# Two instruction streams in a two-layer decoder kernel: one for first halves of a sequence, one for second halves, with the boundary moved by 34 tokens

## The reference

```python
z = x @ w_in                       # q 1024, k 256, v 256, B 512, C 512, h 512, pool 512
a = sliding_window_attention(q, k, v)      # window 128, 16 heads, 4 kv heads, bias and sinks
c = B * causal_conv3(C * h)                # 512 channels
pm = (trailing_mean_2_4_8_16(p) - p) @ pool_w * pool_scale   # reaches 15 rows back
x = LN(alpha * x + concat(a, c, pm) @ w_o)
up = causal_conv3(x @ w_up)                # 2 x 5632 channels
x = LN(alpha * x + (silu(up[:, :5632]) * up[:, 5632:]) @ w_down)
```

## Time and profile before

| | us |
|---|---|
| Three runs | 3389.34, 2963.9, 3504.76 (median 3389.34) |
| The profiled execution, slowest core | 2965.69 |
| Its span, first to last instruction (core 6) | 2963.8 |
| PE busy in it | 2848.2 |
| DVE busy | 1536.0 |
| ACT busy | 962.4 |
| POOL busy | 533.3 |

### The profile page before, as it was taken

The page is one execution under the profiler, slowest core; times in us unless marked ns, Lnnn a source line. Parts: engine busy times, 40 slices in busy tenths (PEclk is TensorE's granted clock), DMA queues, the critical chain, the costliest instruction groups (busy, mean ns, idle before and its releaser), DMA issues.

```text
span 2963.8 us, 53483 instructions; the slowest of 8 cores (2954.7 to 2963.8 us)
## 1 busy us (share of the span) xinstructions
PE 2848.2 (96%) x18644; PEld 1767.7 (60%) x18644; DVE 1536.0 (52%) x3497; ACT 962.4 (32%) x2030; POOL 533.3 (18%) x764
## 2 busy tenths in 40 slices
PE   6999999999999999999999998989999999999995
PEld 3655555555555555555556555756666666666663
DVE  0366447655355435544562564476644563564456
ACT  1466126332033103301363663164311330331136
POOL 2131036100000000000072311261001001000026
PEclk9999999999999999999999999999999999999998
DMA  9522723534433343334448225534444434443434
GB/s 155 100 37 51 193 44 58 84 61 81 79 61 65 66 77 63 66 65 72 72 75 197 43 44 134 103 58 80 75 82 83 81 63 86 74 79 65 86 58 115
DMA packets 86887, 239.30 MB, mean 81 GB/s; under 512 B 11568, under 2 KB 32576, under 8 KB 86080
## 3 DMA queue, kind: packets, MB, share of 16 engines
q0 software_dynamic: 63488, 191.42, 38.7%
q1 hardware_dynamic: 23136, 44.46, 5.0%
HBM read 408.93 MB, written 20.75 MB: 145 GB/s over the span
## 4 chain that ended last, share of the span: by engine, by line
PE 92%; DVE 3%; ACT 2%; issue 1%; DMA 1%; POOL 1%; DVEq 0%; ACTq 0%; POOLq 0%
PE ps L194 92%; DVE xT L194 1%; DMA X<-xg 1%; DVE scr L194 1%; ACT xT L194 1%; ACT scr L194 1%; DMA slab<-w_in 0%; DVE H L194 0%; ACT rstd L194 0%; POOL H L194 0%; POOL xT L194 0%; DVEq L189 0%; DVE rstd L194 0%; ACT L194 0%; DVE small L194 0%
## 5 line engine op out<-in xcount | busy, mean ns | idle before, releaser
L194 PE MATMUL ps<-X,slab 128*128 128x386 bf16 (+6 forms) x10944 | 1747.8, 322 | 33.4 <-DMA slab<-w_in 13.7
L194 PEld LDWEIGHTS ps<-X,slab 128*128 128x128 bf16 x10944 | 1069.4, 98 | 694.7 <-issue 74.4
L194 PE MATMUL ps<-H,slab 128*128 128x384 bf16 (+2 forms) x5760 | 921.3, 319 | 0.0
L194 DVE SCALAR_TENSOR_TENSOR scr<-ps,fcw_s,scr 128x384 f32<-128x384 f32 (+2 forms) x1056 | 628.4, 596 | 406.3 <-ACT scr L194 349.2
L194 PEld LDWEIGHTS ps<-H,slab 128*128 128x128 bf16 x5760 | 564.6, 98 | 329.8 <-issue 2.9
L194 ACT ACTIVATE scr<-ps,fcw_s 128x384 f32<-128x384 f32 (+2 forms) x528 | 296.4, 563 | 1067.9 <-DVE ps L194 737.3
L194 DVE TENSOR_TENSOR xT<-xT,ps 128x384 f32<-128x384 f32 (+3 forms) x549 | 272.2, 531 | 216.1 <-PE ps L194 198.5
L194 POOL DMA_DIRECT2D slab<-w_up x176 | 94.1, 535 | 962.2 <-PE ps L194 960.4
L194 DVE TENSOR_TENSOR H<-scr 128x384 bf16<-128x384 f32 (+4 forms) x278 | 149.2, 539 | 105.7 <-ACT scr L194 76.8
L194 ACT ACTIVATE scr<-xT 128x384 bf16<-128x384 f32 (+2 forms) x192 | 96.8, 506 | 233.7 <-DVE xT L194 196.9
L194 POOL TENSOR_TENSOR H<-H,xT 128x384 f32<-128x384 f32 (+2 forms) x168 | 161.7, 962 | 35.4 <-DVE xT L194 23.8
(11 more groups left out here) (111 smaller groups left out, 938.6 us busy)
## 6 DMA issues: line engine op xcount, KB each, us to landing
slab<-w_up POOLq DMA_DIRECT2D x176, 512.0 KB, 7.7
slab<-w_dn POOLq DMA_DIRECT2D x96, 384.0 KB, 5.5
slab<-w_in POOLq DMA_DIRECT2D x56, 512.0 KB, 11.5
slab<-w_o POOLq DMA_DIRECT2D x32, 512.0 KB, 8.3
xT<-xr SPq DMA_DIRECT2D x16, 580.0 KB, 11.1
xT<-spill SPq DMA_DIRECT2D x16, 516.0 KB, 11.9
slab<-w_dl POOLq DMA_DIRECT2D x16, 512.0 KB, 7.6
xT<-gtab SPq DMA_DIRECT2D x4, 1024.0 KB, 14.0
```

The costliest lines, as they stand in the source:

```text
L194: bi = getattr(engobj, name)(*a_, **k_)
```

## The change

The program is built twice, as `program(0)` for first halves and `program(1)` for second halves, each with its own geometry (a tuple `Geo`, from `geometry(half)`). Each engine loads the word `flag` (0 or 1) from memory at the start and runs one of its two streams. Both streams use the same semaphores and the same tiles.

- **First halves** (even cores): 1058 own tokens instead of 1024. No history is computed: columns start at 256 (`BASE`), groups are 256-640, 640-1024 and 1024-1318 (384, 384, 294 columns) in both layers, also for K. V blocks are 2 to 10. The attention has 9 units per `gp` in both layers, the last with 34 queries. Only the unit at `q0 == 256` is masked; the keys and values of the block in front of it are set to zero in memory, and the two columns in front of the first group of `X_t` too. Conv and pooling don't start 16 columns early. The load of the fourth X piece (columns 0-128) goes. `prat` is still applied.
- **Second halves** (odd cores): 990 own tokens. 260 history columns as before. Groups are 384, 384, 358 columns in layer 0 and 256, 384, 358 in layer 1. V blocks go to 9. The attention has 9 and 8 units per `gp`, the last with 98 queries. No unit is masked, and `prat` isn't applied.
- `smask` and its multiplications go, and the `kmask` load goes. Rows of `X_t` are 1254 columns wide instead of 1288, rows of `xT_t` and `H_t` 1126 instead of 1160. `rden` gets its own memory.

```diff
-H = 260
-NM = 1024
+SHIFT = 34
+NMS = (1024 + SHIFT, 1024 - SHIFT)
-GRP = [[(128, 512), (512, 896), (896, NT)], [(256, 512), (512, 896), (896, NT)]]
-XGR = [(0, 512), (512, 896), (896, NT)]
-XLD = [(128, 512), (512, 896), (896, NT), (0, 128)]
-XW = NT - 128
+def geometry(half):
+    nm = NMS[half]
+    h = 260 if half else 256
+    nt = h + nm + NS
+    if half:
+        g0 = [(128, 512), (512, 896), (896, nt)]
+        g1 = [(256, 512)] + g0[1:]
+        return Geo(h, nm, h + nm, nt, 128, 0, [g0, g1], g0 + [(0, 128)], [[(0, 512)] + g0[1:], [(128, 512)] + g0[1:]])
+    g = [(256, 640), (640, 1024), (1024, nt)]
+    return Geo(h, nm, h + nm, nt, 256, 248, [g, g], g, [g, g])
...
+def emit(nc, flag, progs):
...
+        def both(name, eng):
+            v = eng.value_load(flag, min_val=0, max_val=1)
+            with eng.If(v == 0):
+                progs[0].run(name, eng, esem, dsem)
+            with eng.Else():
+                progs[1].run(name, eng, esem, dsem)
+
+        block.tensor(lambda e: both("pe", e))
+        block.scalar(lambda e: both("act", e))
+        block.vector(lambda e: both("dve", e))
+        block.gpsimd(lambda e: both("pool", e))
+        block.sync(lambda e: both("sp", e))
...
-        load_x(3, 0, 16)
+            if half:
+                load_x(3, 0, 16)
+            else:
+                P.dve(lambda e: e.memset(X_t[:, :, 254 - XB:256 - XB], 0.0), writes=[("X", c, 1) for c in range(16)])
...
-                msk = q0 < 512
+                    msk = not half and q0 == 256
...
-                lo = glo - 16 if gi == 0 else glo
+                    lo = glo - 16 if gi == 0 and half else glo
...
-                if lo <= H - 4 and H <= hi:
-                    P.dve(lambda e: e.tensor_tensor(out=ut[:, 2 + H - 4 - lo:2 + H - lo], in0=ut[:, 2 + H - 4 - lo:2 + H - lo],
-                                                    in1=smask[:, 0:4], op=ALU.mult), reads=["smask", ur], writes=[ur])
...
-                if a <= H and H + 16 <= phi:
+                    if not half and a == H:
...
-                if glo <= H - 4 and H <= hi:
-                    o = H - 4 - glo
-                    P.dve(lambda e, ps=ps, o=o: e.tensor_tensor(out=ps[:, o:o + 4], in0=ps[:, o:o + 4], in1=smask[:, 0:4], op=ALU.mult),
-                          reads=["smask", psr], writes=[psr])
...
-                gate = Xr(15, 0, 128) if l == 0 else []
+                    gate = Xr(15, *XLD[-1]) if l == 0 else []
...
-                load("pool", kmask[:, :], kmask_d, ["kmask"])
+                    if not half:
+                        P.dve(lambda e: e.memset(kmask[:, 0:128], NEG), writes=["kmask"])
+                        P.dve(lambda e: e.memset(kmask[:, 128:256], 0.0), writes=["kmask"])
+                        P.dve(lambda e: e.memset(Kt[:, :, 128:256], 0.0), writes=[("K", 0, 1), ("K", 1, 1)])
+                        P.dve(lambda e: e.memset(V0t[:, 1, :], 0.0), writes=[("V0", 1)])
...
-            KG = ([(0, 512)] if l == 0 else [(128, 512)]) + XGR[1:]
+                KG = geo.KG[l]
...
-            for b in range(KG[0][0] // 128, 11):
+                for b in range(KG[0][0] // 128, LB + 1):
...
-        P.emit()
-        build.stats = P.stats
+            return P
+
+        emit(nc, flag, [program(0), program(1)])
```

More of the change, by code:

```diff
@@ L141, in emit @@
         ins_all.append(fin)
[L142 to L145, removed]
+        self.all = ins_all
         for ins in ins_all:
@@ L149, in emit @@
                 p = ins_all[d]
-                if (not p.dma) and (p.eng != ins.eng or self_hazard(ins, p)):
+                if (not p.dma) and (p.eng != ins.eng or self.self_hazard(ins, p)):
                     p.sig = True
@@ L156, in emit @@
                 ins.val = cnt[ins.eng]
-        per_eng = {e: [] for e in self.ENGS}
+        self.per_eng = {e: [] for e in self.ENGS}
         for ins in ins_all:
[L159 to L209, removed]
@@ new lines, in settle, with self_hazard, run @@
+            self.per_eng[ins.eng].append(ins)
+    def self_hazard(self, ins, p):
+        return ins.eng in ("dve", "act", "pool") and not p.dma and p.eng == ins.eng
+    def run(self, engname, engobj, esem, dsem):
+        waited = {}
+        for ins in self.per_eng[engname]:
+            need = {}
+            for d in ins.deps:
+                p = self.all[d]
+                if p.dma:
+                    key = ("d", p.eng, p.semi)
+                elif p.eng != engname or self.self_hazard(ins, p):
+                    key = ("e", p.eng)
+                else:
+                    continue
+                if p.val > need.get(key, 0):
+                    need[key] = p.val
+            for key, v in need.items():
+                if waited.get(key, 0) >= v:
+                    continue
+                sem = dsem[key[1]][key[2]] if key[0] == "d" else esem[key[1]]
+                engobj.wait_ge(sem, v)
+                waited[key] = v
+            if ins.fn is None:
+                continue
+            name, a_, k_ = ins.fn
+            bi = getattr(engobj, name)(*a_, **k_)
+            if ins.dma:
+                bi.then_inc(dsem[engname][ins.semi], 16)
+            elif ins.sig:
+                bi.then_inc(esem[engname], 1)
@@ L347, in build @@
         small = sb("small", [128, 96])
-        rstd_t = [sb(f"rstd{i}", [128, 392]) for i in range(2)]
+        rden = sb("rden", [128, 512])
+        rstd_t = [sb(f"rstd{i}", [128, 384]) for i in range(2)]
         PSB = [st.enter_context(nc.psum_tensor(f"ps{i}", [128, 512], F32)) for i in range(8)]
[L352 to L377, removed]
@@ new lines, in maybe_reload, with pool_pair @@
+                def maybe_reload():
+                    if not side:
+                        while len(reloaded) < SCRA0 // (XW * 4):
+                            reload(len(reloaded))
+                def pool_pair(i):
+                    sl = SM.get(("in", l, 12 + i))
+                    for t in range(2):
+                        pool_tile(l, 2 * i + t, sl, t)
+                        maybe_reload()
+                    SM.release()
+                pool_pair(1)
+                conv_pair(0)
@@ L1421, in make_in_maps @@
             "s_ffn": np.ascontiguousarray(state_ffn[:, sl].reshape(2, NS * 2, NFT, 128).transpose(0, 3, 2, 1)),
-            "kmask": kmask, "smask": smask, "prat": np.ascontiguousarray(prat.reshape(128, 64)),
-        })
-        for i, (lo, hi) in enumerate(XLD):
-            m[f"xg{i}"] = np.ascontiguousarray(xt[:, :, lo:hi])
+            "flag": np.full((1, 1), half, np.int32),
+            "prat": np.ascontiguousarray(prat.reshape(128, 64)),
+        })
+        for i, w in enumerate(XGW):
+            lo, hi = geo.XLD[i] if i < len(geo.XLD) else (0, 0)
+            m[f"xg{i}"] = padded(xt[:, :, lo:hi], w)
         in_maps.append(m)
```

1717 lines of the change are left out of this document (870 added, 847 removed).

## The result

The changed kernel takes 2840.2 us in the median of its four runs (2839.04, 2839.27, 2841.14 and one of 3332.46), and 2839.3 us without the last. The ratio to the kernel before is 0.958, with a 95% interval of 0.955 to 0.961: 4.2% faster.

A forecast was written before the change was run, and what follows sets the result against it. PE bounds the kernel. Summed terms take 110.0 us off second halves (2962.1 to 2852.1) and 105.0 off first halves (2963.8 to 2858.8); with 1.9 us over the span the forecast is 2861 us, range 2842 to 2890.

The forecast's parts named there:

- The bound and the price of a column: Whole kernel: PE sets the time; a removed column saves 0.41 ns a pass, 77.6 us for 68 columns.
- The other up and down stages: Up and down stages other than up block 0: 42.8 us less on even and odd cores.
- Edits at nothing: Smask multiplications, kmask load, last X load, auxiliary loads and row strides: their changes were costed at no gain.
- block 0: First up block of both layers: 12.5 us less on even and odd cores.
- The mask: One-row mask matmuls in attention: removal saves 21 us on second halves, 12.6 us on first halves.
- The units of 4 queries: Attention on second halves: dropping four tiny units saves 10 us, 5 us off each attention stage.
- The clock: Rival, layer 1's attention: PE's granted clock falls from 0.94 to 0.75, 2909 us; chance 0.11 shared with partial fetch stall.
- The start: Flag load and branch before each engine's first instruction: 3 us added on first halves, 4 us on second halves.
- The norms: Third groups of 294 columns on first halves: PE and DVE level, costing 2 us and up to 8.
- A stall at each packet of code: Rival, instruction fetch inside a branch: PE waits at each packet, 3046 us at 1.2 us each; slower case's chance 0.05.
- The attention's chain of waits: Rival, attention: waits hold it, the mask gives nothing, norms cost 6 us more, 2884 us; chance 0.18.
- Even and odd cores: Rival, balance of the 34 tokens: only one half gets its gain; the sums put the halves 7 us apart.

The follow-up runs named there:

- the slower pace: Changed kernel with the norm's pace beside the last group at 0.5 steps a tile instead of 0.7 on first halves: 2835.6 us against 2839.1.

## Why the prediction was off

- **The bound and the price of a column** held. The other up and down stages lost 43.9 us on both kinds, forecast 42.8. Directly, a down stage of 192 passes lost 7.80 us for 98 columns, 0.415 ns a column; 0.41 was used. The narrower third groups cost no more a column than the wide ones: their matmuls start 126 and 152 ns apart (medians), where 126 and 153 were foreseen. Their rows, core 2 and then core 3, have the forms foreseen:

```profile
L196 PE MATMUL ps<-X,slab 128*128 128x296 bf16 x2816 | 367.8, 289 | 0.0
```
```profile
L196 PE MATMUL ps<-X,slab 128*128 128x360 bf16 x2816 | 442.9, 316 | 0.0
```

- **"Edits at nothing"** is the step that failed. It put the smask multiplications at 0 us, by DVE's busy share in blocks 1 to 3, where DVE is idle half the time. It should have looked at the one stage in which DVE's queue is full, block 0. There they were worth 10.3 us in the kernel before, and 5.6 us (first halves) to 9.5 us (second halves) in the changed one. On second halves that is most of the 13.6 us by which block 0 beat its forecast, on first halves a third to 60% of the 17.4 us. The rest on first halves goes with the widths of the groups and stays open as to its parts. PE's wait "<-POOL H" stood in the earlier trace rows and was put among the norms' waits, without asking what the change does to it.
- **The mask** was right: 23 us measured for all of it where 21 was taken. Idle time did come to light, but in layer 1 only.
- **The units of 4 queries** were right in size (9 to 12 us, forecast 10), though not in place: layer 0 has 2 us of it, forecast 5. That the attention's pace falls with them was in the code and was not costed: 5 us on second halves. Another 8 us there come from edits acting together; the sum added each term by itself. The clock was listed as a rival on the slow side. It moved the other way, from 0.96 to 0.99 in layer 1's attention of second halves.
- **The start** was mis-sized both ways: +3 and +4 us forecast, -1.7 and +8.5 measured. The bound from above, 10 us, held. The one jump per core was foreseen at the start only; the jump at the end of first halves, 3 to 5 us, was missed. The Trainium skill (Runtime: NRT & Kernel Launch, Instruction fetch mechanics) says that a taken branch to code outside the prefetched window stalls until that code is fetched. The traces agree, with 6 to 8 us on GpSimd at the start; that this time is a fetch, they don't show.
- **The norms** cost even cores 4.7 us more than their columns, forecast 2 and up to 8. That DVE is the reason is not borne out by the slower pace, which left these stages as they were. What it is stays open.
- **The rivals.** A stall at each packet of code didn't come: the 2.52 MB of PE's stream are 2.54 MB after, and the long stretches are full. The attention's chain of waits took back part of the mask's price only. Even and odd cores ended 5.6 us apart (medians), forecast 7.
- **The range.** Its lower end took the full mask, no start cost, no norm cost and the best clock, but no gain for the edits costed at nothing; by its own terms it is 2843 us, not 2842. On even cores block 0, the start, q, K and V, and layer 1's attention were off to the fast side, the end and the norms to the slow side. That the time came as near as 2 us to the range is in part luck: the missed jump at the end and the norms hid about 10 us of the gain.

## What to carry to other kernels

An instruction that costs 0.16 us and stands between a matmul and its eviction is priced by the queue in front of it, in the stage in which that queue is longest, and not by its engine's mean share. When columns are removed, ask not only what PE saves but which sums and norms on the slower engines become shorter where PE waits for them. Two streams behind one branch cost one far jump a core, at its start or at its end. The one at the start is the dearer here, so let the lighter stream do it, or issue the first transfers ahead of the branch.

## What the runs showed of the hardware

- A far jump took GpSimd 6 to 8 us at the start (first load at 9.5 to 11.3 us instead of 3.4 us), and 3 to 5 us at the end on first halves. Load of the flag and compare took 1.8 us.
- A matmul of one row between score matmuls of 64 rows spaces both at 0.21 us, where four score matmuls alone take 0.32 us together. Taking 80 of them out was worth 23 us, 0.29 us each, more than their own 0.21 us.
- With half of the cores 6 to 8 us late, the others had their first slab 1.7 us earlier in spite of the flag, most likely because the neighbours were silent.
